# Where the value projection of two cross-attentions is computed: half ahead of time in other attentions' loops, or whole in its own layer

## The reference, cut to what matters

```python
def memory_cross_attention(h, m, w_q, w_kv, w_o, q_norm, k_norm):   # h: 256x1024, m: 256x1024
    q = rms_norm((h @ w_q).reshape(B, S, 4, 128), q_norm)            # w_q: 1024x512
    k, v = _split(m @ w_kv, (512, 512))                              # w_kv: 1024x1024
    k = rms_norm(k.reshape(B, M, 4, 128), k_norm)
    s = einsum('bshd,bmhd->bhsm', q, k) * 128 ** -0.5
    o = einsum('bhsm,bmhd->bshd', softmax(s), v)
    return o @ w_o                                                   # w_o: 512x1024
# per layer i:  x = x + mixer(x);  x = x + memory_cross_attention(norm(x), norm(mem), ...);  x = x + swiglu(norm(x))
```

## Time and profile before

| | |
|---|---|
| median of 3 runs | 2331.09 us (2329.9 to 2332.4) |
| the profiled execution's own time | 2330.88 us |
| its span | 2328.9 us |
| TensorE (PE) busy in the span | 2284.9 us, 98% |
| VectorE (DVE) busy | 1755.5 us, 75% |
| ScalarE (ACT) busy | 544.1 us, 23% |
| granted TensorE clock, mean | 0.998 of full |
| HBM traffic | 203 GB/s mean |

### The profile page before, as it was taken

One profiled execution on the slowest core, in us unless ns is written; L12 is line 12 of the kernel. 1 busy time (PEld: TensorE's weight loads), 2 busy tenths in 40 slices (PEclk: granted clock), 3 DMA queues, 4 the chain that ended last, 5 costly groups with the idle time before them and its releaser, 6 DMA issues.

```text
span 2328.9 us, 44300 instructions
## 1 busy us (share of the span) xinstructions
PE 2284.9 (98%) x17396; PEld 2055.8 (88%) x17396; DVE 1755.5 (75%) x3696; ACT 544.1 (23%) x1379; POOL 190.6 (8%) x298
## 2 busy tenths in 40 slices
PE   8999999999999999999999999999999999999998
PEld 4477999656789997999998799997889998999998
DVE  5866997478579876869986499868869986667883
ACT  2232110027221111212212332122232212213220
POOL 0000001000000010011100011020012100001100
PEclk9999999999999999999999999999999999999999
DMA  6434777741457676468865479664269864446752
GB/s 249 154 128 152 261 277 255 277 171 56 166 208 271 245 270 228 144 215 251 261 251 199 135 236 260 231 224 154 82 188 279 284 251 169 160 168 175 210 180 74
DMA packets 136444, 474.62 MB, mean 204 GB/s; under 512 B 15296, under 2 KB 17472, under 8 KB 135872
## 3 DMA queue, kind: packets, MB, share of 16 engines
q1 hardware_dynamic: 95136, 339.22, 41.1%
q0 software_dynamic: 41120, 132.73, 18.7%
HBM read 470.84 MB, written 1.05 MB: 203 GB/s over the span
## 4 chain that ended last, share of the span: by engine, by line
PE 92%; DVE 4%; ACT 1%; DMA 1%; issue 1%; DVEq 0%; ACTq 0%
PE pair L676 52%; PE bank L676 38%; PE bank L1132 1%; DMA adat<-adaw_dram 1%; PE bank L970 1%; ACT h L1622 1%; DVE rstd L2058 0%; DMA arena<-cmpw_dram 0%; DVE h L2061 0%; DVE arena L2242 0%; DVE arena L3247 0%; ACT rstd L1572 0%; DMA x<-x_in_dram 0%; ACT arena L1634 0%; DVE arena L2935 0%
## 5 line engine op out<-in xcount | busy, mean ns | idle before, releaser
L676 PE MATMUL pair<-arena,ring 128*128 128x128 f32 (+1 forms) x2840 | 389.9, 294 | 4.6 <-issue 2.0
L676 PE MATMUL bank<-arena 128*128 128x128 f32 (+2 forms) x3212 | 379.4, 280 | 3.1 <-DVE arena L2474 0.9
L676 PEld LDWEIGHTS pair<-arena,ring 128*128 128x128 f32 x2840 | 363.4, 192 | 21.1 <-issue 3.6
L676 PEld LDWEIGHTS bank<-arena 128*128 128x128 f32 (+1 forms) x3212 | 360.3, 187 | 18.4 <-issue 8.2
L676 PE MATMUL pair<-arena 128*128 128x128 f32 (+6 forms) x3058 | 347.7, 281 | 3.9 <-DVE arena L2189 1.0
L676 PEld LDWEIGHTS pair<-arena 128*128 128x128 f32 (+4 forms) x3058 | 320.1, 186 | 29.0 <-issue 18.1
L676 PE MATMUL bank<-arena,ring 128*128 128x128 f32 (+1 forms) x2548 | 307.5, 276 | 0.5 <-DVE arena L2242 0.3
L676 PE MATMUL pair<-h,ring 128*128 128x128 f32 (+1 forms) x2048 | 293.2, 298 | 7.9 <-ACT h L1622 5.1
L676 PEld LDWEIGHTS bank<-arena,ring 128*128 128x128 f32 x2548 | 295.7, 192 | 3.0 <-DVE arena L2242 0.7
L676 PEld LDWEIGHTS pair<-h,ring 128*128 128x128 f32 x2048 | 269.8, 192 | 20.8 <-ACT h L1622 5.6
L2641 DVE CUSTOM_DVE_ANT_0 adat<-adat,crow,cols 128x1024 f32<-128x1024 f32 x192 | 243.4, 1279 | 50.3 <-DMA adat<-adaw_dram 50.1
(11 more groups left out here) (307 smaller groups left out, 2486.6 us busy)
## 6 DMA issues: line engine op xcount, KB each, us to landing
ring<-stream_dram SPq DMA_DIRECT2D x638, 512.0 KB, 5.2
adat<-adaw_dram POOLq DMA_DIRECT2D x192, 512.0 KB, 5.2
ring<-stream_dram POOLq DMA_DIRECT2D x80, 256.0 KB, 6.9
arena<-gmrows_dram POOLq DMA_DIRECT2D x1, 2560.0 KB, 10.7
arena<-gmrows_dram POOLq DMA_DIRECT2D x5, 512.0 KB, 7.9
arena<-cmpw_dram POOLq DMA_DIRECT2D x1, 2112.0 KB, 8.8
x<-x_in_dram SPq DMA_DIRECT2D x2, 512.0 KB, 4.5
arena<-mem_in_dram SPq DMA_DIRECT2D x1, 1024.0 KB, 9.1
```

The lines of the kernel that those rows point to most:

```text
L676: return nc.tensor.matmul(out, lhsT, rhs, start=start, stop=stop)
```

## The change

The value projection is no longer cut in two. `memva{i}` and `memvb{i}` become one `memv{i}` of 512 columns (16 products of 512 instead of 16 of 256 in each of two places), computed in the memory layer where `memvb{i}` was. The loops of the mixers keep `memk{i}` alone as filler: two products in each of the 8 steps of layer 0 instead of four, and one in each of the first 13 steps of layer 1. In the memory layer 6 products (before: 8) stand ahead of the turning of q, 4 (before: 3) behind it, and 6 (before: 5) behind the first two units' scores. The order of the weight stream follows; its length does not change.

```diff
-            Linear("memk0", "T", DK, 4, "act"), Linear("memva0", "T", DK, 2, "act"),
+            Linear("memk0", "T", DK, 4, "act"),
             Linear("ab_out", "F", DK, DK, "dve"), Linear("memq0", "T", DK, 4, "dve"),
-            Linear("memvb0", "T", DK, 2, "dve"),
+            Linear("memv0", "T", DK, 4, "dve"),
             Linear("memo0", "F", 4, DK, "dve"), *ffn_tail("0"),
...
-        if lin.name[:5] == "memvb":
+        if lin.name[:4] == "memv":
             places = [[group % 2], [2]]
...
-NSA_LEAD, NSA_FILL = 3, (2, 1, 2, 1, 2, 1, 2, 1, 1, 2, 3, 3, 2, 2, 2, 2)
+NSA_LEAD, NSA_FILL = 3, (1,) * 13
...
-                    lin = PLAN[f"memk{i}" if n < 2 * DK else f"memva{i}"]
+                    lin = PLAN[f"memk{i}"]
...
                 def between(n):
                     if n == 0:
-                        values(DK + 3, TT * DK)
+                        values(DK + 2, TT * DK)
...
-                values(0, DK)
+                values(0, DK - 2)
                 turns(f"memq{i}", "memq_normed", i + 1)
-                values(DK, DK + 3)
+                values(DK - 2, DK + 2)
...
-                def four_products(n):
+                def two_products(n):
                     if n < DK:
-                        for _ in range(4):
+                        for _ in range(2):
                             more()
...
-                lin = PLAN[f"memk{i}" if n < 2 else f"memva{i}"]
-                g, c, w = lin.g0 + n % 2, 512 * (n // 2), lin.N * P
+                lin = PLAN[f"memk{i}"]
+                g = lin.g0 + n
                 act.wait_ge(sem("mm_done"), g + 1)
-                nc.scalar.copy(tm[:, n % 2, c:c + w], banks[SPARE][:, 0:w]).then_inc(sem("freed_act"), 1)
+                nc.scalar.copy(tm[:, n, 0:512], banks[SPARE][:, :]).then_inc(sem("freed_act"), 1)
...
                 def first_between(n):
-                    if n % 2 == 0 and 0 < n <= DK:
-                        memory_out(0, n // 2 - 1)
+                    if n in (4, 8):
+                        memory_out(0, n // 4 - 1)
...
-                    V.tensor_copy(tm[:, t, 768:1024], banks[USED[lin.g0 + t][0]][:, 0:TOK]).then_inc(sem("freed_dve"), 1)
+                    V.tensor_copy(tm[:, t, 512:1024], banks[USED[lin.g0 + t][0]][:, :]).then_inc(sem("freed_dve"), 1)
```

More of the change, by code:

```diff
@@ L68, in make_plan @@
     plan = [Linear("ab_in", "T", DK, 20, "dve"),
-            Linear("memk0", "T", DK, 4, "act"), Linear("memva0", "T", DK, 2, "act"),
+            Linear("memk0", "T", DK, 4, "act"),
             Linear("ab_out", "F", DK, DK, "dve"), Linear("memq0", "T", DK, 4, "dve"),
-            Linear("memvb0", "T", DK, 2, "dve"),
+            Linear("memv0", "T", DK, 4, "dve"),
             Linear("memo0", "F", 4, DK, "dve"), *ffn_tail("0"),
             Linear("nsa_in", "T", DK, 21, "dve"),
-            Linear("memk1", "T", DK, 4, "act"), Linear("memva1", "T", DK, 2, "act"),
+            Linear("memk1", "T", DK, 4, "act"),
             Linear("nsa_out", "F", DK, DK, "dve"), Linear("memq1", "T", DK, 4, "dve"),
-            Linear("memvb1", "T", DK, 2, "dve"),
+            Linear("memv1", "T", DK, 4, "dve"),
             Linear("memo1", "F", 4, DK, "dve"), *ffn_tail("1")]
@@ L99, in make_plan @@
         n = {"F": lin.N, "T": 2 * -(-lin.N // 4), "S": 0, "V": TT, "W": 1}[lin.kind]
-        places = [[SPARE] if lin.name[:5] in ("memk0", "memk1", "memva") or lin.name in LATENT else [(group + i) % 2] for i in range(n)]
-        if lin.name[:5] == "memvb":
+        places = [[SPARE] if lin.name[:4] == "memk" or lin.name in LATENT else [(group + i) % 2] for i in range(n)]
+        if lin.name[:4] == "memv":
             places = [[group % 2], [2]]
@@ L1019, in memory_read @@
             def memory_read(i):
-                lin = PLAN[f"memva{i}"]
+                lin = PLAN[f"memk{i}"]
                 pe.wait_ge(sem("freed_act"), FREER[lin.g0 + lin.groups - 1][1])
@@ L1184, in memory @@
                 linear(f"memq{i}", lambda k: h[:, k, :], h_ready(f"mem{i}", "T"))
-                lin = PLAN[f"memvb{i}"]
+                lin = PLAN[f"memv{i}"]
                 def values(first, end):
@@ L1259, in panels_read @@
                     pe.wait_ge(sem("freed_dve"), FREER[lin.g0 + lin.groups - 1][1])
-                def four_products(n):
+                def two_products(n):
                     if n < DK:
-                        for _ in range(4):
+                        for _ in range(2):
                             more()
                 ahead = projection_ahead("ab_out", U_DSA[1], (4, 5, 6, 7, 0, 1), (2,))
-                stepped_attention(U_MOBA[0], U_DSA[1], four_products, ahead, panels_read)
+                stepped_attention(U_MOBA[0], U_DSA[1], two_products, ahead, panels_read)
                 memory_read(0)
@@ L3450 @@
     for i in range(2):
-        parts[f"memk{i}"], parts[f"memva{i}"], parts[f"memvb{i}"] = np.split(a["mem_w_kv"][i], (512, 768), axis=1)
+        parts[f"memk{i}"], parts[f"memv{i}"] = np.split(a["mem_w_kv"][i], (512,), axis=1)
         parts[f"memq{i}"], parts[f"memo{i}"] = a["mem_w_q"][i], a["mem_w_o"][i]
```

## The result

| | before | after |
|---|---|---|
| median of 8 runs each, same chip | 2330.64 us (2328.75 to 2333.04) | 2337.69 us (2335.91 to 2338.7) |
| the profiled execution's own time | 2330.88 us | 2336.33 us |
| its span | 2328.9 us | 2334.5 us |

The ratio of the medians is 1.0028, with a 95% interval of 1.0019 to 1.0037: 7.05 us slower. Forecast were 2339.6 us, and 2335.0 to 2343.5 as the range.

What follows compares the result with a forecast made beforehand. TensorE, busy 98% of the span, was taken to bound the kernel except where VectorE paces the loops. Loops -1.0 and -3.6, memory layers +11.8 and ring +1.3 gave +8.5 us on 2331.09: 2339.6 us, range 2335.0 to 2343.5.

Steps and rivals of the forecast that it cites:

- Prices: TensorE's cost per product: 0.427 us narrow, 0.853 us wide; 6.83 us per layer move from loop to memory layer.
- Loop of layer 0, -1.0: VectorE paces the early steps; TensorE's values start earlier as VectorE's 1.18 us wait shrinks: 1.0 us gained, bounds 0.7 and 1.2.
- ScalarE's later emptying of the bank: Layer 0's loop, end of step 7: VectorE's squares of k start about 2.3 us later, in idle time; cost taken as 0.
- Loop of layer 1, -3.6: Less fill takes 3.2 us off VectorE's 4.2 us of waits, and 0.4 us goes at the end; bounds 3.0 and 4.6.
- Memory layers, +5.9 each: Fill grows 6.83 us per layer, less a 0.78 us hole and 0.1 us returned; bounds 5.5 and 6.8.
- Rival B: Longer fill hides in the memory layer's 2.73 us of TensorE idling: 4.1 us per layer, 2336.0 us in all; chance 8%.
- One small term: Memory layer: VectorE's bank copy, now of 512 columns, no longer delays the third unit's maxima, returning 0.1 us.
- The ring, +1.3: Behind memo's start, a later-fetched weight slab makes TensorE wait about 1.2 us in layer 0, 0.1 in layer 1.
- The sign named for it: Behind memo0's first addition, VectorE would show a wait for the ring of 2 to 3 us.
- Rival D, the clock: Layer 0's emptier loop drops TensorE to half clock; one spell reaching beyond 119.5 loses 1.5 us, giving 2341.1 us; chance 4%.
- the sign named for D: In layer 0's loop, a granted clock under 1.00 between 100 and 120 us would show the clock falling.
- Sum: Whole kernel: -1.0 - 3.6 + 11.8 + 1.3 = +8.5 us, 2339.6 us.

Runs made afterwards that it cites:

- experiment 1: Changed kernel, with three of memv's four slabs freed one by one as the second token tile's products pass, before memo; 2336.97 us (one run).
- experiment 2: Changed kernel, with v's first 256 columns not computed anywhere and the memory layer's fill at 8, 3 and 5 narrow products; 2326.87 us, ratio to before 0.998.
- experiment 5: The change in layer 0 alone, layer 1 as in the kernel before; 2335.32 us, ratio to before 1.002.
- experiment 6: Kernel before, with the turning of memk (8 transposes) moved from the mixer's output projection to the front of the value products; 2328.57 us, ratio 0.9993.
- experiment 4: Changed kernel, with layer 0's filler in steps 0 to 3 only, four wide products each; 2335.91 us, ratio to before 1.0023.
- experiment 3: Kernel before, with 12 of the 16 value products of each memory layer left out; 2333.3 us, ratio 1.0012.
- experiment 8: Kernel before, with 6 of each memory layer's 16 value products left out, all behind the turning of q; 2330.57 us, ratio 1.0001.

## Why the prediction was right, step by step

- **Prices.** A narrow product 0.427 us, a wide one 0.853: the six wide ones of the changed kernel take 184.82 - 179.67 = 5.15 us, where 5.12 were worked out. Right.
- **Loop of layer 0, -1.0.** Measured -1.06, -1.04 and, from experiments 1 and 2, -1.06 and -1.05. The mechanism held too. In the changed kernel VectorE copies the output at 117.42 to 117.83 and goes straight on to the next maxima at 117.75, where it had waited 1.18 us; TensorE's values start at 117.89. The rest of the 6.83 us went into holes of TensorE in steps 0 to 3: 3.29, 1.27, 1.04 and 1.39 us, where before 1.57 us stood alone. ScalarE's later emptying of the bank cost nothing that shows.
- **Loop of layer 1, -3.6.** Measured -3.62. Its larger part, 3.2 us off VectorE's waits, came out as 4.2 - 1.0. The end of the loop gave 0.3 of the other 0.4: from the last values ahead of it to the first products of the output projection it is 579.37 to 581.49 = 2.12 us, where it was 580.00 to 582.43 = 2.43. These products now wait 0.39 us behind the transposes, and start 0.1 us after VectorE's output copy ends (581.39), which is the wait worked out from the earlier trace rows.

```profile
580.23 0.88 PE L1132 MATMUL bank<-cst,arena 128*128 128x128 f32 x6
581.49 1.96 PE L676 MATMUL pair<-arena,ring 128*128 128x256 f32 x8 [0.39 <-issue]
...
580.97 0.42 DVE L2474 TENSOR_TENSOR arena<-bank,arena 128x256 f32<-128x256 f32 x1
```

- **Memory layers, +5.9 each.** Measured +5.84 in both, +5.83 in experiment 5. Rival B is refuted: only the stretch up to the turning took anything. Experiments 2 and 6 fix the room from both sides: at before's fill the layer takes 20.66 us, and 0.88 us more fit in for nothing. One small term was wrong: no 0.1 us came back from VectorE's bank copy. From the scores behind the last fill to `memo` it is 192.89 to 203.05 = 10.16 us before and 196.01 to 206.17 = 10.16 after. The room was 4.39 - 3.51 = 0.88 us instead (the eight narrow products take 180.71 to 184.22 in experiment 6), not the 0.78 of the bracket, so the two misses cancel.
- **The ring, +1.3.** The sum was nearly right, +1.03, and the chain of waits is the one worked out, as experiment 1 showed. The distribution was wrong, and that the sum came out is luck: 1.2 us were given to layer 0 and 0.1 to layer 1, and 0.09 and 0.94 came. The sign named for it, a wait of 2 to 3 us behind `memo0`'s first addition, was 1.71 there and 2.59 in layer 1. The step at fault is the one that took the landing of the slab from one row a layer of a ring in another order, 4.4 and 3.3 us. In the changed kernel it was 3.2 and 4.1, in experiment 2 3.6 and 4.3, in experiment 4 3.4 and 3.9, and the term follows it: 0.09, 0.46 and 0.27 us in layer 0, 0.94, 1.25 and 0.75 in layer 1. So in this ring layer 1's slab landed later every time. In the ring of the kernel before there was no such order: 4.4 and 3.3, in experiment 3 3.3 and 3.8, in experiment 8 4.3 and 4.3. What sets the landing stays open. I should have given both layers one term with both landings as its bounds; experiment 2, with 1.71 us in all, lies above the forecast.
- **Rival D, the clock.** In the profiled execution of the changed kernel it did not happen, although TensorE's hole grew to 3.29 us. In experiments 1, 2 and 5, with the same loop, it did. This PE row and the windows behind the hole are the changed kernel's:

```profile
101.59 1.18 PE L1132 MATMUL bank<-cst,arena 128*128 128x128 f32 x6 [3.29 <-DVE arena L2457]
...
104.00:110.00 6.00, 4.68 (x32) 2.43 (x30) 5.72 (x22) 2.61 (x10) 0.00 (x0) 1.00 0.00 0
```

And the same place in experiment 2:

```profile
103.02 1.64 PE L1132 MATMUL bank<-cst,arena 128*128 128x128 f32 x6 [3.29 <-DVE arena L2457]
104.45 3.62 PE L676 MATMUL bank<-ring,arena 128*128 128x512 f32 x4
...
103.00:108.00 5.00, 4.99 (x11) 2.21 (x11) 4.72 (x19) 1.70 (x9) 0.00 (x0) 0.50 0.00 0
```

The two wide products took 3.62 us there for 1.88. The loop's length was 51.97 us with the fall (experiment 2) and 51.96 without (the changed kernel): VectorE paces, and a slower TensorE fits into the holes. So a fall costs nothing where VectorE paces, as D said. Its 4% was for a fall that reaches beyond that stretch, and none did (from 113 to 120 the clock was 1.00 in experiments 1, 2 and 5). But the sign named for D, a clock under 1.00 between 100 and 120, came in three of four executions of this loop, which I hadn't foreseen.
- **Sum.** Touched stretches +8.03 beside +8.5; medians +7.05. The remaining 1 us lies within what profiled executions differ by outside the change: the start-up (95.4 to 97.2 us to the first filler in ten executions) and the stretch between the layers (300.8 to 302.5 us).

## What to carry to other kernels

Filler is worth what the waiting engine would otherwise idle in that very step: here 6.83 us of fill cost 1.0 us beside the top-k rounds and 3.9 us in the four steps behind them, and the memory layer, which had room for 0.9 us, charged 5.8 us for the same 6.8. Measure the hole ahead of each releaser before moving work, and move pieces of that size (experiment 6), not whole projections. When a family takes more slabs of a ring, look at when its slabs are freed relative to the next consumer's first need; freeing them one by one gave that term back in the trace. And don't strip hidden fill for tidiness: here a stretch with TensorE busy for 1.04 of 4.40 us was followed by about half the clock (0.56) on work that was on the path.

## What the runs showed of the hardware that was not expected

- Taking 10.2 us of TensorE's work out of the memory layers made the kernel 2.2 us slower (ratio 1.0012, 1.0002 to 1.0021): granted clock 0.56 and 0.57 in spells of 2.4 and 3 us.
- The fall isn't certain for given instructions. The same 1.76 us of idling, with the same work ahead of it, was followed by 1.00 in layer 0 and by 0.58 in layer 1 of one execution (experiment 8). The same hole of 3.3 us was followed by 1.00, 0.66, 0.50 and 0.50 in four executions (the changed kernel, experiments 1, 2 and 5). What decides between them stays open.
- The first 512 KB slab asked for behind a stall landed after 3.2 us in one place and 4.1 in another of one execution, 4.4 and 3.3 in the same places of the kernel before. That spread, about 1 us, is the whole size of the ring's term.
